# Second attention: the turned probabilities of both heads of a step leave PSUM in one copy over two banks instead of two copies

## The reference, cut to what matters

```python
# nsa_attention, per head: selected keys and window keys, each gated
s = einsum('bgrqd,bgqkd->bgrqk', qc, kg) * scale
p = masked_softmax(s, mask)
o = einsum('bgrqk,bgqkd->bgrqd', p, vg)
...
o = g[..., 0:1] * o_cmp + g[..., 1:2] * o_slc + g[..., 2:3] * o_win
# dsa_attention, per block of 128 queries: the 128 best keys by an index score
s = einsum('bqhd,bqkd->bhqk', qb, kg) * scale
p = masked_softmax(s, mask)
o = einsum('bhqk,bqkd->bqhd', p, vg)
# then
o = concatenate([o_nsa, o_dsa], axis=-1) @ w_out
```

## Time and profile before

| | |
|---|---|
| time, median of 3 runs | 1860.96 us (1859.05 to 1862.5) |
| the profiled execution | 1861.72 us, of which the span is 1859.9 us |
| busy share of the span | PE 97%, POOL 65%, DVE 63%, ACT 20% |
| chain that ended last | PE 71%, POOL 12%, issue 7%, DVE 6% |
| second attention | from 1311.8 us (first scores) to 1427.3 us (first matmul of the output projection) |
| its instructions | 96 copies L1701, 96 exponentials L1706, 240 transposes L1265, 192 scores L1254, 192 values L1285 |

### The profile page before, as it was taken

The page is one execution under the profiler, slowest core; times in us unless marked ns, Lnnn a source line. Parts: engine busy times, 40 slices in busy tenths (PEclk is TensorE's granted clock), DMA queues, the critical chain, the costliest instruction groups (busy, mean ns, idle before and its releaser), DMA issues.

```text
span 1859.9 us, 24399 instructions
## 1 busy us (share of the span) xinstructions
PE 1799.1 (97%) x8626; PEld 1415.5 (76%) x8626; DVE 1177.7 (63%) x1715; ACT 376.6 (20%) x801; POOL 1215.7 (65%) x1182
## 2 busy tenths in 40 slices
PE   6999999999999999999999999999999899999997
PEld 3788888887865688878888888778545687888785
DVE  6888658874684312578823876799884987007613
ACT  2111000001215511121100001444786110001001
POOL 3477677685565277757777768947563948668761
PEclk8999999999999999999999999999999899999998
DMA  8555454542221022445525542513010222232221
GB/s 309 180 181 169 158 195 162 192 141 82 77 83 57 1 89 93 136 135 187 169 85 176 179 155 93 115 53 116 14 33 1 91 69 91 91 109 94 90 91 46
DMA packets 224505, 213.34 MB, mean 115 GB/s; under 512 B 22385, under 2 KB 220206, under 8 KB 224430
## 3 DMA queue, kind: packets, MB, share of 16 engines
q1 hardware_dynamic: 223376, 211.70, 35.5%
q10 hardware_dynamic: 1054, 0.66, 0.1%
HBM read 210.25 MB, written 2.10 MB: 114 GB/s over the span
## 4 chain that ended last, share of the span: by engine, by line
PE 71%; POOL 12%; issue 7%; DVE 6%; DMA 2%; ACT 1%; ACTq 0%; POOLq 0%; DVEq 0%; SPq 0%
PE ps L735 19%; PE ps L736 19%; PE ps L737 19%; POOL w_lo L669 7%; PE ps L1254 2%; PE ps L1265 2%; POOL w_hi L664 2%; PE ps L1285 2%; POOL w_hi L663 1%; PE ps L1056 1%; DVE ada_sum L1815 1%; DMA raw<-in_ffn_w_gate 1%; PE ps L758 1%; PE ps L1077 1%; PE ps L1065 1%
## 5 line engine op out<-in xcount | busy, mean ns | idle before, releaser
L669 POOL TENSOR_TENSOR w_lo<-raw,w_hi 128x512 fp32r<-128x512 f32 (+3 forms) x580 | 764.4, 1347 | 11.9
L735 PE MATMUL ps<-h_hi,w_hi 128*128 128x512 f32 (+1 forms) x1248 | 490.4, 393 | 1.6 <-DVE h_lo L2324 1.4
L737 PE MATMUL ps<-h_hi,w_lo 128*128 128x512 f32 (+1 forms) x1248 | 487.0, 390 | 0.0
L736 PE MATMUL ps<-h_lo,w_hi 128*128 128x512 f32 (+1 forms) x1248 | 486.7, 390 | 0.0
L661 POOL TENSOR_TENSOR w_hi<-raw,ones 128x8 fp32r<-128x8 f32 x145 | 34.2, 236 | 504.0 <-PE ps L737 412.9
L1815 DVE SCALAR_TENSOR_TENSOR ada_sum<-ada,cT,ada_sum 128x256 f32<-128x256 f32 x378 | 325.9, 862 | 13.4
L735 PEld LDWEIGHTS ps<-h_hi,w_hi 128*128 128x128 f32 (+1 forms) x1248 | 234.7, 188 | 55.1 <-issue 4.8
L737 PEld LDWEIGHTS ps<-h_hi,w_lo 128*128 128x128 f32 (+1 forms) x1248 | 234.6, 188 | 50.0
L736 PEld LDWEIGHTS ps<-h_lo,w_hi 128*128 128x128 f32 (+1 forms) x1248 | 234.7, 188 | 48.1
L735 PE MATMUL ps<-g_hi,w_hi 128*128 128x512 f32 x608 | 237.9, 391 | 3.3 <-ACT sg L1733 3.2
L737 PE MATMUL ps<-g_hi,w_lo 128*128 128x512 f32 x608 | 236.7, 389 | 0.0
(11 more groups left out here) (364 smaller groups left out, 2350.7 us busy)
## 6 DMA issues: line engine op xcount, KB each, us to landing
ada<-in_ada_w SPq DMA_DIRECT2D x31, 1024.0 KB, 5.2
ada<-in_w_ada SPq DMA_DIRECT2D x24, 1024.0 KB, 6.7
raw<-in_ffn_w_gate SPq DMA_DIRECT2D x22, 1024.0 KB, 6.7
raw<-in_ffn_w_up SPq DMA_DIRECT2D x22, 1024.0 KB, 5.1
raw<-in_w_in SPq DMA_DIRECT2D x16, 1024.0 KB, 5.2
raw<-in_w_up SPq DMA_DIRECT2D x16, 1024.0 KB, 5.3
raw<-in_w_down SPq DMA_DIRECT2D x16, 1024.0 KB, 5.0
raw<-in_ffn_w_down SPq DMA_DIRECT2D x16, 768.0 KB, 4.4
```

What stands on the lines that cost most here:

```text
L669: last = pool.tensor_tensor(lo[:, c], src[:, c], hi[:, c].bitcast(F32), ALU.subtract)
L735: pe.matmul(o, wh, xh, start=start, stop=False)
L736: pe.matmul(o, wh, xl, start=False, stop=False)
L737: return pe.matmul(o, wl, xh, start=False, stop=stop)
```

## The change

Each step's two copies out of PSUM become one. The two heads' tiles lie in neighbouring banks (2 and 3), and the two places in `pt2` lie a constant distance apart (`PT_SLOT`), so that one instruction with an extra dimension of two reads both banks and writes both places. It waits for the transposes of both heads, and counts 2 on `at_ev` when it is done. `pt2` gets 128 more columns so that the slice of the new form stays inside the buffer; what is written to it is the same as before. PE, DVE and POOL keep their instructions and waits.

```diff
-    pt2 = place("pt2", [P, 4 * PT_SLOT + 256], at=at(40))
+    pt2 = place("pt2", [P, 4 * PT_SLOT + 384], at=at(40))
...
-        def pair_turn(t):
-            qc, pi = t // 2 % 4, t // 8
-            act.wait_ge(at_tr, PAIR_T0 + t + 1)
+        def pair_turn(s):
+
+            pi, qc = divmod(s, 4)
+            act.wait_ge(at_tr, PAIR_T0 + 2 * s + 2)
             if pi >= 2:
                 act.wait_ge(pr_pv, pi - 1)
-            dst = turned(t)(P * qc, PT_ROW * (qc + 1)).rearrange("p (c q) -> p c q", q=PT_ROW)[:, :, 0:P]
-            act.copy(dst, ps[:, B_T2[t % 2], 0:P * (qc + 1)].rearrange("p (c q) -> p c q", q=P)).then_inc(at_ev, 1)
+            first = 2 * PT_SLOT * (pi % 2) + P * qc
+            both = pt2[:, first:first + 2 * PT_SLOT].rearrange("p (h n) -> p h n", n=PT_SLOT)
+            dst = both[:, :, 0:PT_ROW * (qc + 1)].rearrange("p h (c q) -> p h c q", q=PT_ROW)[:, :, :, 0:P]
+            src = ps[:, B_T2[0]:B_T2[0] + 2, 0:P * (qc + 1)].rearrange("p h (c q) -> p h c q", q=P)
+            act.copy(dst, src).then_inc(at_ev, 2)
...
-            for t in (2 * (s - LAG_T), 2 * (s - LAG_T) + 1):
-                if 0 <= t < 2 * PAIR_STEPS:
-                    pair_turn(t)
+            if 0 <= s - LAG_T < PAIR_STEPS:
+                pair_turn(s - LAG_T)
```

## The result

The changed kernel takes 1864.26 us (median of 14 runs, 1860.04 to 1864.92). The kernel before, in its 14 runs of the same comparison, takes 1861.20 (1858.43 to 1862.5). The ratio is 1.0021, 95% interval [1.0014, 1.0028], so the change costs 2.6 to 5.2 us by these runs; the two medians themselves lie 3.06 us apart. A second comparison of the same two kernels gave 1.0015 [1.0006, 1.0024]. The kernel is slightly slower, by about the 0.2% at which the prediction drew its line. Single executions far outside a kernel's spread (2299.02 and 3604.63 us of `fill_merged`, 2579.2 us of the kernel before beside it) are in no ratio.

A forecast was written before the change was run, and what follows sets the result against it. PE was taken to bound the kernel, so later copies cost only in fill and drain: 0.3 + 0 (body) + 1.4 = 1.7 us on the median 1860.96 gives 1862.7 us. The range over all cases was 1859.5 to 1866.

The forecast's parts named there:

- the likeliest case: Whole kernel: the forecast itself, a later end through fill and drain, 1861.9 to 1863.9 us, given a chance of 0.56.
- merged copies: ACT's joined copies in the second attention: 0.38, 0.59, 0.80 and 1.02 us for blocks 0 to 3.
- body: Middle of the second attention, PE never idle: the later copy stays hidden, costing 0 to 0.2 us, taken as 0.
- transposes 45: Drain: PE's transposes of step 45 wait for merged copy 44 and start 0.37 us later.
- transposes 46: Drain: PE's transposes of step 46 wait for copy 45, queued behind late exponentials, and start 0.55 us later.
- transposes 47: Drain: PE's transposes of step 47 wait for merged copy 46 and start 0.99 us later.
- last values: End of the drain: PE's last values wait for merged copy 47 and start 1.39 us later.
- drain: After the last scores of the second attention: the delayed links cost 1.4 us, with nothing behind to win it back.
- fill: First steps of the second attention: transposes 4 start 0.3 us later, and this loss stays.
- the tightest place: Body, between copy 40 and transposes 41: 0.15 us to spare against 0.06 to 0.15 needed for PE's reaction.
- a pair takes more than 8.50 us: Body: sign that the forecast is wrong; a pair of steps was expected to keep taking 8.50 us.
- My rival: Drain: longer PE idle time drops the clock to half, losing 1.5 us in the projection, 1864.2 us; chance 0.07.

The follow-up runs named there:

- fill_merged, Experiment 5: The changed kernel with merged copies only in steps 0 to 3, two copies from step 4 on; fill 26.76 us, ratio 1.0006 to the kernel before.
- Experiment 6: The changed kernel plus one ACT copy of 128 columns ahead of the merged copy in turns of steps 4 to 42; body 79.61 us, ratio 1.0010.
- Experiments 3 and 8: The kernel before: 3 makes side 0's copy wait for both heads' transposes, drain 11.10 us; 8 moves turn 47's chunk read one turn later on ACT and DVE, 9.75.
- tail_order: The kernel before with turn 47's finished-chunk read moved one turn later on ACT and DVE; drain 9.75 us, median 1858.81, ratio 0.9997.
- read_later: The kernel before with ACT's `h_hi` read in turns 15 to 47 moved one turn later, DVE left alone; body 81.73 us, drain 10.81, ratio 1.0020.

## Why the prediction held, point by point

The forecast was 1862.7, and 1861.9 to 1863.9 for the likeliest case; measured were 1864.26 and 1863.63. The first lies above that case's bounds and inside the whole range (up to 1866). The sign, the mechanism and the place were right. The size was too small: 1.7 us, against 3.06 and 2.56 between the medians. The stages say how much of that is the change's.

| term of the sum | predicted | measured |
|---|---|---|
| merged copies, us | 0.38, 0.59, 0.80, 1.02 | 0.37, 0.58, 0.80, 1.01 |
| body | 0 to 0.2 | 0.00 |
| transposes 45, after 44 | +0.37 | +0.45 |
| transposes 46 | +0.55 | +0.57 |
| transposes 47 | +0.99 | +1.08 |
| last values | +1.39 | +1.47 |
| drain | +1.4 | +1.47 |
| fill, same half clock | +0.3 | +0.41 to +0.53 (3.4 + 3.4), +0.58 (10.2), +0.35 to +0.45 (13.7) |
| sum of the stages | +1.7 | +1.8 to +2.05 |

*What the merge saves.* ACT's interval from copy 44 to the next instruction is now 0.27 us (1415.55 to 1415.82), where two copies took 0.32: 0.05 saved, as worked out. It has no buyer in the body.

*Body.* Hidden, and the tightest place was named rightly. In the changed kernel copy 40 ends 0.14 us before transposes 41, and 0.14 to 0.15 is also what lies between a copy's end and transposes that wait for it, in the drain below. Experiment 6 shows that there is nothing beyond it. One reading was wrong: that a pair takes 8.50 us everywhere. Of the nine pairs from transposes 8 to 44 three take 9.36 us, before as after, because PE has four more matmuls there (L1270), and 6 x 8.50 + 3 x 9.36 = 79.08. The prediction's sign "a pair takes more than 8.50 us" is to be read as more than the same pair took before.

*Drain.* The chain ran link by link as forecast. Experiments 3 and 8 take out one link each (8 in the kernel before), and each gives back the amount that was expected. The missing 0.08 us are reaction times: copies 43, 46 and 47 start 0.08 to 0.09 us after the transposes they wait for, where I had 0.05, and transposes 45 and 47 start 0.14 to 0.15 us after the copy's end, where I had 0.10. The last values follow the copy by 0.05, near the 0.06 forecast.

*Fill.* This term was mis-sized: 0.3 forecast, 0.41 to 0.58 in the two patterns of half clock that the first profiles had. Experiment 5 has the pattern from which I worked. Counted from the first scores, transposes 2 came 0.16 us later there than in the kernel before, transposes 3 0.10 later, and transposes 4 0.45 later. The first two are as forecast. The step that failed is the last one, for which I had added 0.2: transposes 3 took 1.33 us in place of 1.24, copy 3 started 0.09 us after them in place of 0.05, and transposes 4 another 0.14 to 0.15 after the copy in place of 0.10:

```profile
1326.47 1.33 PE L1265 MATMUL ps<-kst,p 128*128 128x128 f32 x8
...
1329.05 0.42 PE L1265 MATMUL ps<-kst,p 128*128 128x128 f32 x2 [0.19 <-POOL p L712]
```

The row names POOL, whose scaling ended last by the profile. But copy 3 ends at 1327.89 + 1.01 = 1328.90, and transposes 4 follow it by 0.14 to 0.15 us in all seven profiles with merged copies in the first steps, whenever POOL ended. With two copies they start at least 0.31 after it. Under 10.2 us of half clock the loss comes from two waits, before transposes 3 and before transposes 4. The changed kernel's first profile has both:

```profile
1323.51 1.07 PE L1265 MATMUL ps<-kst,p 128*128 128x128 f32 x8 [0.19 <-ACT pt L1705]
...
1325.82 0.43 PE L1265 MATMUL ps<-kst,p 128*128 128x128 f32 x2 [0.19 <-ACT pt L1705]
```

*The clock.* My rival put a fall of the clock into the drain. PE ran there at full clock in every profile. It is in the fill that the half clock's length varies, 6.8, 10.2 or 13.7 us, and the longest costs 1.3 to 1.5 us over the one of 10.2 (28.04 against 26.77 in the changed kernel; 27.69 against 26.19 with two copies). It came in 4 of the 7 profiles with merged copies in the first steps, and in 1 of the 7 with two copies there. If merging made it more frequent in that proportion, that would add (4/7 - 1/7) x 1.3 = 0.6 us to the mean, and the sum would be 2.4 to 2.6 us, near what both sets of times show. With seven profiles each this is not shown. One thing speaks against it. Half clock begins before the first of the copies, which comes 9.5 to 10.0 us after the first scores. Where it began 3.30 to 3.42 us after the first scores it lasted 13.7 us, four times with merged copies and once (`tail_order`) without. Where it began 3.46 to 3.60 us after them it lasted 10.2 (three times) or 3.4 + 3.4 (`read_later`), and from 4.79 on always 3.4 + 3.4. So the moment at which it begins, which lies before any copy, parts the stretches of 13.7 us from the others in all 14 profiles, whatever the form. That, too, is a reading of few profiles, and the limit between 3.42 and 3.46 us is thin. It stays open whether the rest of the difference is this or only spread; the first comparison's 2.6 to 5.2 us lies above the 2 us that the stages prove, the second's 1.1 to 4.5 holds it.

*The rule on breaking up.* The Trainium skill (Perfetto Trace Analysis, section Optimizing Scalar/DVE Operations) says that breaking instructions up may let work finish sooner where ScalarE isn't saturated but makes others wait. The trace agrees: joining them cost 1.47 us in the drain.

## What to carry to other kernels

Joining two instructions of a side engine saves only the fixed part of the interval that the second one takes on the engine, here 0.05 us, and not its duration of 0.28 to 0.59; and it delays the first half's start and the first half's release. Price it where the pipeline fills and drains, link by link from the rows, and look in the body for the one place with the least slack. When an instruction moves on one engine, look for the engine that stands waiting for its result with other work queued behind.

## What was not expected of the hardware

Equal code at full clock is very regular. The body is 79.08 or 79.09 us in 12 of 14 profiles (all but the two kernels that lengthen it), and the drain of one form repeats within 0.01 us. Yet one kernel's executions spread over 4 to 5 us (1858.43 to 1862.5, 1860.04 to 1864.92). What differs between the profiles is where and how long PE runs at half clock. The two first profiles, for instance, differ by 3.4 us when they reach the attention, in code that is the same. Between 1170 and 1190 us of the span, where 0.8 of the 3.4 us arise, the granted clock averages 0.83 in the kernel before and 0.91 in the changed one. From 1290 us to the attention PE is busy without a gap in both, and 1.6 more arise:

```profile
1290.00:1311.80 21.80, 21.80 (x146) 18.66 (x145) 19.90 (x42) 6.71 (x13) 6.03 (x5) 0.84 0.22 65
```

```profile
1290.00:1308.40 18.40, 18.40 (x130) 15.62 (x130) 17.61 (x36) 6.03 (x11) 4.26 (x3) 0.91 0.22 59
```

A granted clock of 0.84 over 21.80 us is 7.0 us at half clock, and 0.91 over 18.40 us is 3.3. At half clock PE does half the work, so the difference of 3.7 us costs about 1.8, close to the 1.6 found by setting the same matmuls of the two traces side by side, as were the 0.8. Such differences also part the executions of a set: of the first comparison's 14, six of the kernel before stayed below 1860.2 us, and one of the changed kernel did. Whether that is chance or comes of the change is not shown.

A change worth 2 us must be read from its stages, in profiles with the same pattern of the clock.
